# Stepping the slices of the activations by 16 bytes from one to the next

## The reference

```
for layer in range(2):
    xn = rms_norm(h, g);  proj = xn @ w_in            # 1024 x 2560
    h = h + concat(ssm, spatial gating, differential attention)(proj) @ w_out
    xn = rms_norm(h, g);  h = h + conv_gated_mlp(xn)  # 1024 -> 2 x 2816 -> 1024
h = rms_norm(x, g_pre) @ w_in_2                       # queries, keys, values, gates
x = x + rms_norm((sum of three gated branches) @ w_out_2, g_post)
```

## Time and profile before

| | before |
|---|---|
| median of 3 runs | 965.48 us |
| span of the profiled execution | 964.3 us |
| PE busy | 953.3 us (99%) |
| DVE busy | 687.4 us (71%) |
| ACT busy | 567.6 us (59%) |
| POOL busy | 232.1 us (24%) |
| DMA queue of the weights | 54.9% |

### The profile page before, as it was taken

The page is one execution under the profiler, slowest core; times in us unless marked ns, Lnnn a source line. Parts: engine busy times, 40 slices in busy tenths (PEclk is TensorE's granted clock), DMA queues, the critical chain, the costliest instruction groups (busy, mean ns, idle before and its releaser), DMA issues.

```text
span 964.3 us, 15784 instructions
## 1 busy us (share of the span) xinstructions
PE 953.3 (99%) x6119; PEld 837.1 (87%) x6123; DVE 687.4 (71%) x1081; ACT 567.6 (59%) x960; POOL 232.1 (24%) x189
## 2 busy tenths in 40 slices
PE   8999999999999999999999999999999999999997
PEld 6887899999888888899999988999778889888886
DVE  7987878786765877857777754748576755666885
ACT  7967666676855657756666544535454445555733
POOL 5560203536500110302445500021131300000030
PEclk9999999999999999999999999999999999999999
DMA  8642466656664634466566565665545445754462
GB/s 299 227 131 68 142 219 186 189 178 184 194 197 152 180 127 153 133 188 192 180 194 178 195 196 154 216 202 173 166 139 153 153 144 170 199 162 155 154 180 82
DMA packets 48618, 165.96 MB, mean 172 GB/s; under 512 B 6560, under 2 KB 7072, under 8 KB 48544
## 3 DMA queue, kind: packets, MB, share of 16 engines
q1 hardware_dynamic: 48544, 164.95, 54.9%
HBM read 162.83 MB, written 1.05 MB: 170 GB/s over the span
## 4 chain that ended last, share of the span: by engine, by line
PE 88%; ACT 4%; POOL 3%; DVE 3%; issue 1%; DMA 1%; SPq 0%; DVEq 0%; POOLq 0%; ACTq 0%
PE PJ L655 14%; PE PJ L657 13%; PE PJ L656 13%; PE PJ L648 10%; PE PJ L647 10%; PE PJ L646 10%; PE PJ L593 2%; PE PJ L603 2%; PE PJ L586 2%; PE T L1118 1%; ACT sm L1378 1%; PE T L1109 1%; ACT whi L1177 1%; DMA raw<-weights_in 1%; DVE wlo L1873 1%
## 5 line engine op out<-in xcount | busy, mean ns | idle before, releaser
L1873 DVE TENSOR_TENSOR wlo<-raw,whi 128x1024 fp32r<-128x1024 f32 x294 | 368.7, 1284 | 87.2 <-ACT whi L1177 84.8
L1177 ACT ACTIVATE whi<-raw 128x1024 fp32r<-128x1024 f32 x294 | 301.6, 1059 | 64.9 <-DMA raw<-weights_in 62.5
L646 PE MATMUL PJ<-xthb,whi 128*128 128x256 f32 x832 | 233.7, 281 | 0.0
L648 PE MATMUL PJ<-xthb,wlo 128*128 128x256 f32 x832 | 233.4, 281 | 0.0
L647 PE MATMUL PJ<-xtlb,whi 128*128 128x256 f32 x832 | 232.4, 279 | 0.0
L655 PE MATMUL PJ<-whi,xthb 128*128 128x512 f32 (+1 forms) x424 | 170.8, 403 | 0.3 <-DVE wlo L1873 0.2
L657 PE MATMUL PJ<-whi,xtlb 128*128 128x512 f32 (+1 forms) x424 | 164.0, 387 | 0.0
L656 PE MATMUL PJ<-wlo,xthb 128*128 128x512 f32 (+1 forms) x424 | 164.0, 387 | 0.0
L647 PEld LDWEIGHTS PJ<-xtlb,whi 128*128 128x128 f32 x832 | 157.0, 189 | 0.3
L646 PEld LDWEIGHTS PJ<-xthb,whi 128*128 128x128 f32 x832 | 157.0, 189 | 0.3
L648 PEld LDWEIGHTS PJ<-xthb,wlo 128*128 128x128 f32 x832 | 156.9, 189 | 0.0
(11 more groups left out here) (419 smaller groups left out, 1353.2 us busy)
## 6 DMA issues: line engine op xcount, KB each, us to landing
raw<-weights_in SPq DMA_DIRECT2D x294, 512.0 KB, 3.6
rt<-bmerge_in SPq DMA_DIRECT2D x6, 256.0 KB, 4.1
memx<-mem_in SPq DMA_DIRECT2D x2, 512.0 KB, 4.0
y_out<-xn SPq DMA_DIRECT2D x4, 256.0 KB, 2.3
rowv<-rows_in SPq DMA_DIRECT2D x1, 576.0 KB, 10.5
xres<-x_in SPq DMA_DIRECT2D x2, 256.0 KB, 3.0
xres<-x_in SPq DMA_DIRECT2D x1, 512.0 KB, 7.7
ptmp<-bexp_in SPq DMA_DIRECT2D x2, 256.0 KB, 6.0
```

Source lines behind the costliest of these rows:

```text
L646: pe.matmul(o, a, xh[:, k, :], start=(first and f % 2 == 0), stop=False, skip_group_check=True)
L648: m = pe.matmul(o, b, xh[:, k, :], start=False, stop=last, skip_group_check=True)
L1177: act.activation(whi[:, p % HIGHS, :], raw[:, p % LOADS, :], ACT.Copy).then_inc(hi_ready, 1)
L1873: dve.tensor_tensor(wlo[:, p % LOADS, :], raw[:, p % LOADS, :], whi[:, p % HIGHS, :].bitcast(F32), ALU.subtract).then_inc(lo_ready, 1)
```

## The change

The slices of `xthb` and `xtlb` are 260 elements apart instead of 256 (`SLICE = TOK + 4`), so slice k lies 16k bytes further on within 512 bytes than slice 0. The same is done with `hth`, not with `htl`. The start offsets of `xth`, `xtl`, `fth` and `ftl` within their tensors are new. `lines` goes; `lines1` moves behind `hth` and shrinks from 96 to 72 elements, `lines2` shrinks from 96 to 64. The instructions, their order and their waits are the same; only addresses and the steps between slices differ.

```
+SLICE = TOK + 4
-        xthb = sbt(ctx, "xthb", [P, KD * TOK + 128], F32R)
-        xtlb = sbt(ctx, "xtlb", [P, KD * TOK + 16], F32R)
-        (xth, xtl), (fth, ftl) = ([b[:, o:o + KD * TOK].rearrange("p (k n) -> p k n", k=KD) for b in (xthb, xtlb)]
-                                  for o in (0, 8))
+        xthb, xtlb = (sbt(ctx, n, [P, KD * SLICE + 112], F32R) for n in ("xthb", "xtlb"))
+        (xth, xtl), (fth, ftl) = ([b[:, o:o + KD * SLICE].rearrange("p (k n) -> p k n", k=KD)[:, :, 0:TOK]
+                                   for b, o in zip((xthb, xtlb), at)] for at in ((112, 96), (0, 112)))
-        sbt(ctx, "lines", [P, 120])
-        sbt(ffs, "lines1", [P, 96])
-        hth = sbt(ffs, "hth", [P, FT, TOK], F32R)
+        hthb = sbt(ffs, "hthb", [P, FT, SLICE], F32R)
+        hth = hthb[:, :, 0:TOK]
+        sbt(ffs, "lines1", [P, 72])
-        sbt(two, "lines2", [P, 96])
+        sbt(two, "lines2", [P, 64])
```

## The result

The changed kernel takes 972.28 us (971.58 to 972.34) against 965.52 us before: a ratio of 1.0065, 95% interval 1.0053 to 1.0077, so by the ratio 6.3 us slower (the medians lie 6.8 us apart). The forecast was 3.5 us less, 962.0. The span of the profiled execution went from 964.3 to 970.5 us.

What follows compares the result with a forecast made beforehand. TensorE was taken as the bound, time being matmul count times pitch. Gains of 2.9, 1.1, 0.8 and 0.7 us less losses of 1.0 and 1.0 made 3.5 us, from 965.48 to 962.0 us; range 954 to 974.

Steps and rivals of the forecast that it cites:

- D: Place of a matmul's stationary operand less that of its moving one, in bytes; the slice's place in token form, its negative in feature form.
- The surplus of the token form at D <= -32, taken as 8.6 ns: Slice stationary: pitch above 213.3 ns set at 8.6, the middle of 10.6 and 6.8, bounds 2.3 and 20.0.
- mirror image of +32: Token form at negative D: the 6.6 ns loss at +32 turned into a gain, 13.4 - 6.6 = 6.8 ns.
- gains of 2.6 us (`hth`, `htl`, `oth`): Token form: `hth` gains 1.1 us on 352 matmuls, `htl` 0.8 on 176, `oth`/`otl` 0.7 on 144.
- the gain of 2.9 us on `xth`: `xth`/`xtl` in token form, 1440 matmuls: surplus from 15.4 to 13.4 ns, 2.0 ns each.
- unsettled matmuls: Token form at place 0 just behind other work, 230 ns before settling to 227; they add 2.0 ns to `xth`'s mean before.
- The feature form at D <= -32, taken as 10.6: Slice moving: pitch above 106.7 ns set at 10.6 for all D <= -32, from the rows at place 32.
- forecast loss of 1.0 us: `xth`/`xtl` in feature form, 480 matmuls: surplus rises from 13.4 to 15.4 ns.
- Rival 1: Token form never settles because D moves every 6 matmuls; with feature-form losses 7.6 us slower, 973.1 us; chance 0.2.
- Rival 2: Feature form: far distances cost more than -32, up-projection loses 3.5 or 6.8 us more; 971 to 975 us; chance 0.12.
- Rival 3: Larger gain: surplus falls 6.6 ns per 32 bytes to a floor of 2.3; 955 us; chance 0.2.
- Rival 4: Nothing: gains and losses cancel, or pitch differences come from something other than addresses; 965.5 us; chance 0.13.

Runs made afterwards that it cites:

- e3_head64: Kernel before with 64 unread bytes ahead of `whi`, so every operand moves by 64 bytes and distances stay: 965.83 us, ratio 0.9998.
- e1_still: Kernel before with the changed kernel's places held constant, no steps between slices, `fth` and `ftl` at 112: 962.63 us, ratio to before 0.9965.
- e7_probe: Kernel before with constant places `xth` 64, `fth` 400, `hth`/`htl` 128, `oth`/`otl` 256, `memh`/`meml` 416: 969.51 us in one run.
- e10_step256: Kernel before with `memh`/`meml` slices 1280 bytes apart (places 0 and 256), `xth` at constant 256, `fth` at constant 368: 958.84 us in one run.
- e2_fth64: Kernel before with `fth` and `ftl` 64 bytes instead of 32 into their tensors, nothing else: 966.67 us, ratio 1.0010.
- e6_fth112: Kernel before with `fth` and `ftl` at 112 instead of 32, and `xtlb` 16 elements longer: 958.21 us, ratio 0.9924.
- e5_best: Kernel before with constant places `fth`/`ftl` at 112, `xth`/`xtl` and `memh`/`meml` at 448, all else at 0: 957.25 us, ratio 0.9911.

## Why the prediction was wrong

The basis held: the time is a count of matmuls times pitches, pitches follow the distance of slice and weights (e3_head64), writers and waits cost nothing, and 1 ns is worth 4.8 us. L1506 takes 623 ns after the change against 624. The pitches did follow D. The sign was lost in one step.

- *The surplus of the token form at D <= -32, taken as 8.6 ns.* It was a middle between the feature form's 10.6 and a mirror image of +32. Measured: 20.0 ns at -32 (`oth` in the changed kernel), 20.0 for `hth` and `htl` at 224 and 352 (e1_still), 18.9 for the down-projection as changed. There is no slope through 0 and no mirror. 0 (with 256) is the bottom of a narrow dip (13.4 ns); from 32 bytes on, near and far on both sides, constant places are at 19 to 21, and 448, with 15.5 to 16, is the only lower one of those run. This turned gains of 2.6 us (`hth`, `htl`, `oth`) into a loss of 3.6, and the gain of 2.9 us on `xth` into a loss of 3.1: 12.2 us of error, of which the feature form gave 2.5 back (next points). The upper bound of 20.0 that the prediction gave for this price was the value: with it in the place of 8.6, its formula gives 17.6 for `xth` in token form, where 231.0 ns, 17.7, were measured, and 19.1 for `hth`, and the whole sum would have been 9.3 us slower instead of 3.5 faster.
- *A term put at nothing without a reason.* For `xth` in token form the sum sets 15.4 before, of which 2.0 are unsettled matmuls, against 13.4 after, with no unsettled ones. The whole gain of 2.9 us is these 2.0 ns; 2.9 of the 3.5 us forecast rested on them. Without them the forecast would have been a gain of 0.6 us. That the term vanishes away from place 0 turned out about right (`xth` at a constant 64 in e7_probe is at 233.3 ns over all its matmuls, and 233.3 is also the settled value there), but nothing on record then said so.
- *That both forms share one curve of D*, because they agree at 0. Of the places run in both forms they agree there alone: at place 32 and 64 feature form is below its value at 0, token form above its own.
- *The feature form at D <= -32, taken as 10.6.* The mean over all stepped slices of `fth` is near the forecast (117.5 against 117.8 ns), by accident: the six slices from 32 to 112 run at 116.3, 118.4, 113.5, 119.2, 120.0 and 113.3. For `xth` the forecast loss of 1.0 us was a gain of 0.9: its slices at -64 to -32, where D is positive and the forecast had 126.7 ns, run at 113.6 to 118.9 in the three chunks of 96 matmuls, under the 119.9 of place 0.
- *Rival 1* had the right sign and nearly the time (973.1 against 972.3), and the row that it watched came out (a down-projection above 228). Its mechanism, settling lost by stepping, is refuted for the down-projection by e1_still, where nothing steps and the pitch is 233. The rows that carried it, show how a stretch at place 0 begins and say nothing of steps; e10_step256 steps and stays at 226.7. That its time came so near is in part luck: it had 2.0 us of feature-form losses that did not come, and left out the branch products and the memory, which lost 1.1. Some settling between steps is there (the two slices at 230.7 and 228.7 ns above), but the down-projection is no slower with steps (232.2) than without (233.0 on average in e1_still). *Rival 2*, that far distances cost more than -32 in feature form, had the sign too and not the mechanism: the slices of `fth` from 48 to 112 have a surplus of 10.2 ns on average, and the up-projection lost 0.4 us, not 3.5 or more. Its 971 to 975 us also need the gains of all tensors in token form to be lost; with those of the down-projection alone, as it says, its terms give 967 to 971. *Rival 3*'s floor of 2.3 ns rested on a row that was misread: L798 issues four float32 matmuls and the trace shows eight records in that stretch, six of them in the earlier trace rows, so 216 ns is not the pitch of a whole one. No pitch came near it. *Rival 4* and the Trainium skill's rule of independent ports ("TensorE: Matmul & The Clock Gate", section "Step-by-step: what each phase is for") would have made all of these kernels equal; they differ by 15 us with identical instructions, so this case does not bear out that addresses would not matter.

The trace of before had no token-form row at any place but 0 and 32, and the one at 32 was the worst of its kind. The only row of this form away from 0 said "away from 0 it is worse"; I used the sign of D, and a row of the other form, to argue it away.

## What to carry to other kernels

When a matmul stream is bound by TensorE alone, with a new stationary operand for every matmul, read pitches start to start, by tensor, and list them beside each operand's address distance modulo 256 bytes. Here the kernels with the same instructions lie 1.6% apart, and the pitches of one form up to 6%. Don't interpolate between places and don't carry a value from one form to the other: give each tensor a constant place and try several in one kernel, since each tensor is a probe of its own. Spreading slices over many places buys about the average, which here was worse than the place that the token form already had; the gain was in one offset of the feature form.

## What the runs showed of the hardware

Surplus: pitch less 106.7 or 213.3 ns (256 or 512 columns over 2.4 GHz), at constant places modulo 256, in settled stretches:

| place | feature form (slice moves, 256 columns) | token form (slice stationary, 512 columns) |
|---|---|---|
| 0 | 13.3 | 13.4 |
| 32 | 10.0 or 11.1 | 20.0 |
| 64 | 11.1 | 20.0 |
| 96 | 13.2 | 21.0 |
| 112 | 6.6 | not run long |
| 128 | not run | 19.0 |
| 144 (400) | 6.6, 10.0 or 12.0 | not run |
| 160 (416) | 12.1 | 20.0 |
| 192 (448) | 6.6 or 11.1 | 15.5 to 16 |
| 224 (480) | not run | 20.0 |

The rows come from these kernels: 0 and 32 from that before (token form at 32 from 12 matmuls alone); 64 from e2_fth64 and e7_probe; 96 from e1_still and the changed kernel; 112 from e1_still and e6_fth112; 128, 144 and 160 from e7_probe, one run; 192 from e1_still and e5_best; 224 from the changed kernel and e1_still.

Three things were unexpected. The same place can hold more than one lasting pattern: 116.7 and 117.8 ns at 32, 116.7, 118.7 and 113.3 at 400, and 113.3 and 117.8 at 448 (e5_best: the memory's last 48 matmuls and the last 48 of `xth` in feature form run at 117.8). Adding the same 64 bytes under everything changes no pitch. And apart from these patterns the pitches come out alike from kernel to kernel where the places agree: to 0.1 ns in the down-projection (226.8 in all eight kernels that have it at place 0), to 0.2 in `xth`, to 0.4 in the short stretches of the branch products. What causes the dependence on the distance, and what selects a pattern, was not found; the table is all that the runs show, and it was measured with float32r operands only.
